# Per-token norm statistics by matrix products with a column of ones, early split of the next layer's first weight chunks, output turned unscaled and stored by token tile

## What is computed

```python
xn  = rmsnorm(x, norm_w) * (1 + scale) + shift      # shift, scale, gate from SiLU(cond) @ w_mod[l] + b_mod[l]
P   = xn @ w_in[l]                                  # split among attention, convolution and gated linear attention
x   = x + gate * concat(A, B, C) @ w_out[l]         # A, B, C: the three groups' outputs, 2048 channels
y   = rmsnorm(x, final_norm_w)                      # after both layers
```

## Time and profile before

| | us |
|---|---|
| median of three runs | 2360.26 |
| lowest of them | 2359.84 |
| highest of them | 12316.95 |
| the profiled execution, its own time | 2355.74 |
| its span, first to last instruction | 2353.9 |

### The profile page before, as it was taken

The page is one execution under the profiler, slowest core; times in us unless marked ns, Lnnn a source line. Parts: engine busy times, 40 slices in busy tenths (PEclk is TensorE's granted clock), DMA queues, the critical chain, the costliest instruction groups (busy, mean ns, idle before and its releaser), DMA issues.

```text
span 2353.9 us, 33174 instructions
## 1 busy us (share of the span) xinstructions
PE 2236.4 (95%) x13019; PEld 1936.6 (82%) x13019; DVE 1307.4 (56%) x2555; ACT 670.2 (28%) x1034; POOL 191.2 (8%) x128
## 2 busy tenths in 40 slices
PE   5999999999999998989969999999999999998996
PEld 3588888888888987889968888888888898788995
DVE  5387787982445445556457554565244454465634
ACT  4232222221332223333133222232133332343313
POOL 0000000000000000422321000000000000042231
PEclk9999999999999999999979999999999999999998
DMA  9998666663323224443444536454322222445343
GB/s 358 378 297 273 212 225 215 218 209 89 95 64 86 87 78 159 148 155 122 117 123 147 188 120 183 137 152 133 89 86 72 86 87 78 144 151 171 121 127 110
DMA packets 351564, 358.25 MB, mean 152 GB/s; under 512 B 16198, under 2 KB 258716, under 8 KB 350812
## 3 DMA queue, kind: packets, MB, share of 16 engines
q1 hardware_dynamic: 321328, 313.19, 42.8%
q10 hardware_dynamic: 30124, 43.51, 5.1%
HBM read 297.77 MB, written 58.88 MB: 152 GB/s over the span
## 4 chain that ended last, share of the span: by engine, by line
PE 88%; DVE 4%; DMA 3%; ACT 2%; issue 1%; SPq 1%; ACTq 0%; POOL 0%; POOLq 0%; DVEq 0%
PE psP L687 29%; PE psP L722 19%; PE psP L739 9%; PE psT L697 7%; PE psO L890 5%; PE psO L864 3%; PE psP L824 2%; PE psT L834 2%; PE psT L890 1%; PE psO L649 1%; PE psO L751 1%; DMA proj_scratch<-stage 1%; PE psO L846 1%; PE psT L606 1%; PE psP L825 1%
## 5 line engine op out<-in xcount | busy, mean ns | idle before, releaser
L687 PE MATMUL psP<-x_high,high 128*128 128x512 f32 x1024 | 410.1, 400 | 17.8 <-DVE x_low L1548 15.5
L687 PE MATMUL psP<-x_high,low 128*128 128x512 f32 x1024 | 400.6, 391 | 0.0
L687 PE MATMUL psP<-x_low,high 128*128 128x512 f32 x1024 | 400.2, 391 | 0.0
L1500 DVE SCALAR_TENSOR_TENSOR macc<-mraw,cond,macc 128x384 f32<-128x384 f32 (+1 forms) x960 | 389.7, 481 | 0.0
L1084 ACT ACTIVATE high<-raw 128x1024 fp32r<-128x1024 f32 x128 | 135.1, 1058 | 519.9 <-PE psT L697 510.1
L687 PEld LDWEIGHTS psP<-x_high,high 128*128 128x128 f32 x1024 | 193.1, 189 | 70.6 <-issue 27.1
L722 PE MATMUL psP<-x_high,high 128*128 128x320 f32 x1024 | 246.2, 322 | 0.5 <-issue 0.5
L722 PE MATMUL psP<-x_low,high 128*128 128x320 f32 x1024 | 235.1, 311 | 0.0
L722 PE MATMUL psP<-x_high,low 128*128 128x320 f32 x1024 | 235.1, 311 | 0.0
L687 PEld LDWEIGHTS psP<-x_high,low 128*128 128x128 f32 x1024 | 193.0, 189 | 41.8
L687 PEld LDWEIGHTS psP<-x_low,high 128*128 128x128 f32 x1024 | 193.4, 189 | 40.4 <-issue 1.9
(11 more groups left out here) (273 smaller groups left out, 3425.8 us busy)
## 6 DMA issues: line engine op xcount, KB each, us to landing
raw<-in_w_in_dram SPq DMA_DIRECT2D x128, 512.0 KB, 4.8
wmod<-in_w_mod_dram SPq DMA_DIRECT2D x32, 1024.0 KB, 9.6
mraw<-in_w_mod_dram SPq DMA_DIRECT2D x64, 512.0 KB, 4.4
mraw<-in_w_mod_dram SPq DMA_DIRECT2D x32, 1024.0 KB, 7.3
raw<-in_w_in_dram SPq DMA_DIRECT2D x32, 1024.0 KB, 6.0
raw<-in_w_out_dram SPq DMA_DIRECT2D x64, 512.0 KB, 4.5
old<-x_scratch SPq DMA_DIRECT2D x64, 320.0 KB, 3.1
proj_scratch<-stage ACTq DMA_DIRECT2D x64, 256.0 KB, 3.1
```

The source lines that it names most:

```text
L687: mm = pe.matmul(latent_ps[m], w[:, kk, cols], x[:, k, 0:DEC], start=(k == 0 and w is whole and x is x_high), stop=(k == KT - 1 and w is r ...
L1500: m = dve.scalar_tensor_tensor(acc[:, v, 0:width], mraw[hf][:, k, 0:width], c, acc[:, v, 0:width], ALU.mult, ALU.add)
```

## The change

It does the following.

- **Statistics by token.** POOL adds only 15 squares. PE makes, for each of the five token tiles, the product of `sq_sum`'s 128 x 128 block (as the stationary operand) with one column of ones: `token_sums`, right behind the last output tile. `last_sums` adds the same five products from tile 15's square. The result is 128 x 5, tokens on the partitions. DVE makes variance, ACT a square root (`root`), DVE the reciprocal and a Newton step (`token_factor`) on 128 x 5.
- **Seam.** DVE writes five diagonal matrices of the factors, PE spreads them by ones to `rstd_ps` in PSUM, DVE scales tiles 0 and 1 from there and copies it to `rstd` only after splitting them. The fence becomes an arrival; SP waits for all four as before, POOL later than before. Chunks 0 and 1 of layer 1 are cast by ACT around tile 14's square and their lows made by DVE before tile 15 is added; chunks 2 and 3 are cast between the shifts.
- **End.** In layer 1's output loop DVE multiplies each tile by the final norm's weight (`weigh`) once it has been squared. PE turns the unscaled tiles into seven banks of PSUM, four transposes each, token tile by token tile; ACT takes the even banks, DVE the odd ones, each multiplying by the token's factor as a scalar by partition. SP stores half the channels of one token tile at a time: 10 DMAs of 512 KB.

```diff
+        token_ps, rstd_ps = psO[:, 0:TT], psO[:, 0:TOK]
+        y_banks = [bank[:, at:at + 512] for bank, at in ((psT, 0), (psT, 512), (psP[0], 0), (psP[0], 512), (psP[1], 0),
+                                                         (psP[1], 512), (psO, 512))]
...
-            for q in range(4):
-                part = slice(q * D // 4, (q + 1) * D // 4)
-                sp.wait_ge(s["x_taken"], KT + (q + 1) * KT // 4)
-                for i in range(TT):
+            for i in range(TT):
+                for side in range(2):
+                    part = slice(side * D // 2, (side + 1) * D // 2)
+                    sp.wait_ge(s["x_taken"], KT + 2 * i + side + 1)
+                    sp.wait_ge(s["y_scaled"], KT + 2 * i + side + 1)
                     dst = io["y_sample"][0, i * P:(i + 1) * P, part] if i < TT - 1 else io["y_prompt"][0][:, part]
                     sp.dma_start(dst, ytok[:, i, part]).then_inc(s["y_out"], 16)
-            sp.wait_ge(s["y_out"], 16 * TT * 4)
+            sp.wait_ge(s["y_out"], 16 * TT * 2)
...
+            def token_sums(l):
+
+                pe.wait_ge(s["x_acc"], (l + 1) * KT + SEED)
+                for i in range(TT):
+                    pe.matmul(token_ps[:, i:i + 1], sq_sum[:, i * P:(i + 1) * P], ones[:, 0:1], start=(i == 0), stop=False,
+                              skip_group_check=True)
+
+            def last_sums(l):
+
+                pe.wait_ge(s["x_sq"], (l + 1) * KT)
+                for i in range(TT):
+                    mm = pe.matmul(token_ps[:, i:i + 1], xt[1][:, i * P:(i + 1) * P], ones[:, 0:1], start=False,
+                                   stop=(i == TT - 1), skip_group_check=True)
+                mm.then_inc(s["stat_summed"], 1)
...
-                    fence(pe, FENCES * l)
+                    token_sums(l - 1)
+                    last_sums(l - 1)
+                    arrive(pe)
+                    pe.wait_ge(s["x_squared"], 2 * TT + 2 + l * TT)
                     spread(psO, ones[:], sq_sum).then_inc(s["stat_summed"], 1)
...
+            token_sums(DEPTH - 1)
+            for u in range(TT * 4):
+                i, q = u // 4, u % 4
+                if u == 2:
+                    last_sums(DEPTH - 1)
+                    for slot in range(2):
+                        pe.wait_ge(s[f"taken{slot}"], DEPTH * per_layer + SEED)
+                if u < 4:
+                    pe.wait_ge(s["y_scaled"], 4 * q + 4)
+                if u >= len(y_banks):
+                    before = u - len(y_banks)
+                    pe.wait_ge(s["y_scaled" if before % 2 else "x_taken"], KT + before // 2 + 1)
+                for k in range(4):
+                    mm = pe.transpose(y_banks[u % len(y_banks)][:, k * P:(k + 1) * P], xf[:, 4 * q + k, i * P:(i + 1) * P],
+                                      ident[:])
                 mm.then_inc(s["embed_turned"], 1)
...
+            def root(n):
+
+                act.wait_ge(s["stat_var"], n + 1)
+                act.activation(x_tmp[:], x_var[:], ACT.Sqrt).then_inc(s["stat_exp"], 1)
...
+                elif l > 0:
+                    act.wait_ge(s[f"tile_done{n // 2}"], l * per_layer - 1 + n % 2 + SEED)
+                act.activation(ring(high, n), ring(raw, n), ACT.Copy).then_inc(s["chunk_cast"], 1)
...
-                    fence(act, FENCES * l)
-                    ln_exp(r_a[:], rstd[:], r_b[:], "stat_var", l + 1, "stat_exp")
+                    root(l)
...
-                    for n in range(RING):
-                        cast_chunk(n)
...
+                    if k in (1, 3):
+                        cast_chunk(2 + k // 2)
...
+                with act.Fori(0, OUT_PAIRS - 1) as i:
                     for slot in range(2):
...
+                        square(i, slot)
                 act.wait_ge(s["g_saved"], 32 * PAIRS * (l + 1) + SEED)
...
+                for slot in range(2):
+                    if l + 1 < DEPTH and slot == 0:
+                        cast_ring(l + 1, 0)
+                    square(OUT_PAIRS - 1, slot)
+                    if l + 1 < DEPTH and slot == 0:
+                        cast_ring(l + 1, 1)
+                if l + 1 < DEPTH:
+                    arrive(act)
+
+            root(DEPTH)
+            act.wait_ge(s["stat_rs"], STAT_AT[DEPTH] + 4)
+            for u in range(0, TT * 4, 2):
+                i, q = u // 4, u % 4
+                act.wait_ge(s["embed_turned"], KT + u + 1)
+                act.activation(ytok[:, i, q * 512:(q + 1) * 512], y_banks[u % len(y_banks)], ACT.Identity,
+                               scale=x_rs[:, i:i + 1]).then_inc(s["x_taken"], 1)
...
-            def norm_factor(stat, n):
-
-                dve.wait_ge(s["stat_summed"], n + 1)
-                dve.tensor_scalar(r_a[:], stat[:, 0:TOK], 1.0 / D, EPS, ALU.mult, ALU.add).then_inc(s["stat_var"], 1)
-                refine(rstd[:], r_a[:], r_b[:], sq_sum[:], "stat_exp", n + 1, "stat_rs", 3 * n)\
-                    .then_inc(s["stat_rs"], 1)
-                dve.wait_ge(s["stat_rs"], 3 * n + 3)
+            def token_factor(n):
+
+                base = STAT_AT[n]
+                dve.wait_ge(s["stat_summed"], 2 * n)
+                dve.tensor_scalar(x_var[:], token_ps, 1.0 / D, EPS, ALU.mult, ALU.add).then_inc(s["stat_var"], 1)
+                dve.wait_ge(s["stat_exp"], 2 + n)
+                dve.reciprocal(x_r0[:], x_tmp[:]).then_inc(s["stat_rs"], 1)
...
+                dve.wait_ge(s["stat_rs"], base + 3)
+                dve.scalar_tensor_tensor(x_rs[:], x_tmp[:], 1.5, x_r0[:], ALU.add, ALU.mult).then_inc(s["stat_rs"], 1)
+                dve.wait_ge(s["stat_rs"], base + 4)
...
-                    norm_factor(psO, l)
+                    token_factor(l)
+                    for i in range(TT):
+                        dve.tensor_scalar(sq_sum[:, i * P:(i + 1) * P], ident[:], x_rs[:, i:i + 1], None, ALU.mult)\
+                            .then_inc(s["x_squared"], 1)
+                    dve.wait_ge(s["stat_summed"], 2 * l + 1)
+                    for slot in range(2):
+                        dve.tensor_tensor(xt[slot][:], xf[:, slot, :], rstd_ps, ALU.mult).then_inc(s[f"scaled{slot}"], 1)
+                    arrive(dve)
...
-                    scale_even(0)
-                    for n in range(2):
-                        chunk_low(n)
-                for i in range(KT // 2) if l > 0 else ():
+                    for slot in range(2):
+                        split_x(slot, 0)
+                    dve.tensor_copy(rstd[:], rstd_ps).then_inc(s["stat_rs"], 1)
+                    dve.wait_ge(s["stat_rs"], STAT_AT[l] + 5)
+                    scale_even(1)
+                    chunk_low(2)
+                for i in range(1, KT // 2) if l > 0 else ():
...
+                def weigh(j):
+
+                    dve.wait_ge(s["x_sq"], j + (l * KT + 1))
+                    tile = xf[:, bass.ds(j, 1), :].rearrange("p a b -> p (a b)")
+                    dve.tensor_scalar(tile, tile, head[:, bass.ds(j + 2 * KT, 1)], None, ALU.mult).then_inc(s["y_scaled"], 1)
...
                     for f in range(4):
+                        if last and f == 3 and l + 1 < DEPTH:
+                            ring_low(l + 1, 0)
+                            ring_low(l + 1, 1)
...
+                        if l + 1 == DEPTH and f > 0:
+                            weigh(i * 4 + (f - 1))
+                    if l + 1 == DEPTH:
+                        weigh(i * 4 + 3)
...
+            token_factor(DEPTH)
+            for u in range(1, TT * 4, 2):
+                i, q = u // 4, u % 4
+                dve.wait_ge(s["embed_turned"], KT + u + 1)
+                dve.tensor_scalar(ytok[:, i, q * 512:(q + 1) * 512], y_banks[u % len(y_banks)], x_rs[:, i:i + 1], None,
+                                  ALU.mult).then_inc(s["y_scaled"], 1)
...
-                    fence(pool, FENCES * l)
-                    pool.wait_ge(s["stat_rs"], 3 * l + 3)
-                for i in range(KT // 2) if l > 0 else ():
+                    arrive(pool)
+                    pool.wait_ge(s["stat_rs"], STAT_AT[l] + 5)
+                for i in range(1, KT // 2) if l > 0 else ():
...
+                if l > 0:
+                    pool.wait_ge(s["phase_over"], 4 * FENCES * l)
...
+                add_square(OUT_PAIRS - 1, 0)
```

More of the change, by code:

```diff
@@ L66 @@
 SLOT_FILLS = [3, 4, 4, 4]
+STAT_AT = [0, 3, 8]
 OUT_PAIRS = KT // 2
@@ L1074, in _ @@
                 if l > 0:
-                    fence(act, FENCES * l)
-                    ln_exp(r_a[:], rstd[:], r_b[:], "stat_var", l + 1, "stat_exp")
+                    root(l)
                 def cast_chunk(n):
[L1080 to L1084, removed]
+                    cast_ring(l, n)
                 def take_group(g):
@@ L1360, in _, with square @@
                 keep_sum(2 * FILL - 1)
-                with act.Fori(0, OUT_PAIRS) as i:
+                def square(i, slot):
+                    act.wait_ge(s[f"taken{slot}"], i + (occ + SECOND + 1 + SEED))
```

(40 more changed lines are left out.)

15 lines of the change are left out of this document (12 added, 3 removed).

## The result

The changed kernel takes 2332.3 us (median of four runs, 2330.16 to 2334.39) against 2360.98 beside it: a ratio of 0.988, interval 0.9861 to 0.9899, a gain of 28.7 us. In a later comparison (after_again) the same code took 2335.58 against 2360.44, 0.9902 (0.9881 to 0.9923), a gain of 24.9.

What follows compares the result with a forecast made beforehand. TensorE's matrix products were taken to set the pace, with gains only where it idles: seam 7.3 plus end 12.8 made 20.1 us, so 2335.6 profiled and, with 4.5 carried over, 2340.2 us; range 2334 to 2348.

Steps and rivals of the forecast that it cites:

- Table load and root: At seam and end, after the variance: one load of 1.28, root 0.2, handovers 0.1, all in the path.
- The stream, kept at 17.0: At the end, from the first store's issue to the end of the span: 17.0 us, as before the change.
- My own bound: At the end: 0.4 us more gain if the two microseconds of stores at 309 GB/s were made good.
- Small steps at the end: From tile 15's square to the factor: last sums 1.2, variance 0.25, load and root 1.6, reciprocal 0.2, refining 0.6.
- Seam, the other terms: Between the layers, the chain's steps besides load and root; the first product of layer 1 was to start 7.3 us earlier.
- the cheap price: At the seam, the last sums' five products at full clock: 1.2 us.
- the dear end: At the seam, the last sums at half clock: 1.1 us more than the 1.2 taken.
- Costed at nothing: Early casts and lows, GpSimd's addition, later loads, x tiles 2 and 3, and weighing: hidden beside other work.
- a given-back seam gain: Rival, chance 0.07: TensorE starts layer 1 earlier, then waits for x tiles; all 7.3 us go, time 2347.5.
- the slower one: Rival, chance 0.05: weighing in layer 1's output loop exceeds VectorE's idle 4.17 us per tile by 1.26, eating 20.1.
- its lower end: The range's lower limit, 2334 us: best bounds with the clock full, gain 23, and 3 us of scatter between runs.
- Carrying over 4.5 us: The median of runs before, 2360.26, lay 4.5 above the profiled execution; added to 2335.6 it gave 2340.2.

Runs made afterwards that it cites:

- The two experiments on the load: Changed kernel with two fulfilled waits ahead of each square root: 2338.4 us; kernel before with a tiny copy behind each fence: 2355.15 us.
- e2_end: The kernel before with only the end of the changed kernel, its seam left as it was: 2342.9 us, ratio 0.9928.
- e7_warm: The changed kernel with 29 products that nobody reads put on TensorE at the seam: 2331.09 us, ratio 0.9884.
- e10_best: The changed kernel with 29 unread filler products at the seam and, after the first token tile, stores of whole 8 KB rows: 2329.88 us, ratio 0.9876.

## Why the prediction missed, step by step

- **Table load and root, 1.6 at each place: mis-sized.** The root with its handover is 0.24 (1204.96 to 1205.20), and the load is off the path: 1.36 too much at each place, 1.28 of it the load. The step that failed is that I laid the load end to end with the root and gave no overlap with the last sums a chance. The two experiments on the load move this term by itself, in both directions. I had read the load's place in before, behind the variance, as belonging to the function. I had set the rule of the Trainium skill, "ScalarE: Activation LUTs", section "Table sets: the hidden batching unit", against the count of loads only; it asked for a gain 2.6 us smaller, and the miss was 2.6 us the other way. The loads counted as forecast, one at each place; their place was wrong. The trace of before held the counterexample, in an attention head on the timeline, where the load runs at once and its logarithm waits on for 2.61 us:

```profile
581.91 1.28 ACT L1036 ACT_TABLE_LOAD   x1
585.80 0.21 ACT L1036 ACTIVATE qb<-qv 128x5 f32<-128x5 f32 x1 [2.61 <-DVE qr L1661]
```

- **The stream, kept at 17.0: mis-sized by 1.8.** My own bound allowed 0.4 for the slow stretch. What isn't the form of the stores was worth 1.0 (17.01 against 16.05 with rows of 2 KB; its cause is open), and the longer rows in larger DMAs 0.8, which I had not priced at all; the rows of 384 GB/s were rows of 2 KB.
- **Small steps at the end: 0.2 too much.** From the square's end to the factor 2.6 us were measured, 4.05 forecast, 1.28 of the difference the load.
- **Seam, the other terms: right, within 0.2 each.** The last square ended 1.78 after its addition began, against 1.94; last sums 1.38 against 1.2; refining to the first read 4.3 against 4.35, at half clock as assumed; scaling to the first product 4.9 against 4.9. That the last sums met the cheap price was luck. In after_again they took 2.06, near the dear end (1.2 + 1.1), and over nine executions they took 1.28 to 2.06, each behind 0.86 us of idle time:

```profile
1200.11 2.06 PE L772 MATMUL psO<-ones,r_b 128*128 128x1 f32 x10 [0.86 <-ACT r_b L1407]
```

- **Costed at nothing: right.** The lows ended 2.4 us before the addition, TensorE waited for no x tile after the first product of layer 1, and output tiles kept their 7.04, but for one wait of 0.7 us for a low of w_out at 2212, which neither profile of before has (0.2 in after_again, none in e2_end). The rival of a given-back seam gain did not come, nor did the slower one.
- **The range: its lower end was the error.** It took a best gain of 23 and 3 us of scatter. The gain is 24.7 (seam 8.6, end 16.1), beyond that bound, since the load was priced without a lower end at both places. With the level of after_again the time, 2335.58, would have lain inside the range although the mechanism failed: that it fell below 2334 took the 3.3 us of the next point as well.
- **From profile to median.** Carrying over 4.5 us was sound as far as it went: the first profile of before was 4.3 short in a stretch that the change leaves alone. 2360.26 - 24.7 = 2335.6, and after_again measured 2335.58. The first median, 2332.3, is 3.3 lower. Medians of the kernel before lie between 2356.71 and 2360.98 in the comparisons here, so a difference of this size occurs between comparisons of one program; which wait made it in those runs is open, since one execution alone was profiled.

In sum: of the 7.9 us between 2340.2 and 2332.3, 2.6 are table loads, 1.8 the stream, 0.2 small steps, and 3.3 the level of that comparison.

## What to carry over

A setup instruction such as a table load is priced by where its waits and the instruction before it let it start: read what stands ahead of the load and what it waits for, and look through the whole trace for a place where it already ran early. A stream of stores is priced by production first and then by the form of its DMAs. Before a sum is made against one profiled execution, divide it into stretches: one that the change leaves alone and that is a few us short against another execution is scatter.

## What the runs showed of the hardware

- VectorE's low of a chunk (128x1024) takes longer while GpSimd works: 1.18 with GpSimd idle, 1.90 where it adds a square for the first half, 2.58 while it scales an x tile.
- Store streams moved 377, 399 and 422 GB/s with rows of 2, 4 and 8 KB, in DMAs of 256, 512 and 1024 KB (one window each).
- The clock's fall has no fixed place in the program. The same ten records of the last sums took 1.28 (e7_warm), 1.38, 2.06 and, in e10_best, 1.78 us, all behind the same 0.86 us of idle time. Filler products that began at full clock shortened the seam to 11.83 us; those that began at half delayed the ones product by 1.7 us. One execution stands for each.
